# Moving operands of a matmul laid out line by line, three chunks interleaved, at a set distance from the weights

## What is computed

```python
# first block: T = 256 tokens, D = 2048
z = rmsnorm(x, g_mix) @ w_in                       # conv inputs, q, k, v, forget logits, gates
x = x + (gc * (conv_y @ w_conv_out) + ga * (attn @ w_attn_out)) @ w_mix_out
x = x + square(relu(rmsnorm(x, g_mlp) @ w_ff1)) @ w_ff2      # D_FF = 8192
x = rmsnorm(x, g_final)
# second block: shift, scale and gate come from silu(c) @ w_ada + b_ada
p = (rms_norm(x, g) * (1 + scale_m) + shift_m) @ w_in_2      # q, k, v, xs, z, B, C, dt
x = x + gate_m * (concat([rms_norm(moba_attention(q, k, v)), ssd_mixer(xs, z, B, C, dt)]) @ w_out_2)
h = rms_norm(x, g_ffn) * (1 + scale_f) + shift_f
x = x + gate_f * (conv_ffn(h, w_up, w_down))                 # FFN_DIM = 5632
out = rms_norm(x, g)
```

## Time and profile before

| | |
|---|---|
| time, median of 3 runs | 2489.05 us (2488.6 to 2489.89) |
| profiled execution | 2489.22 us, span 2487.4 us |
| TensorE (PE) busy | 2465.1 us, 99% |
| VectorE (DVE) busy | 1971.3 us, 79% |
| ScalarE (ACT) busy | 1263.9 us, 51% |
| mean granted TensorE clock | 0.999 |
| DMA | 567 MB, 228 GB/s over the span |

### The profile page before, as it was taken

The page is one execution under the profiler, slowest core; times in us unless marked ns, Lnnn a source line. Parts: engine busy times, 40 slices in busy tenths (PEclk is TensorE's granted clock), DMA queues, the critical chain, the costliest instruction groups (busy, mean ns, idle before and its releaser), DMA issues.

```text
span 2487.4 us, 46915 instructions
## 1 busy us (share of the span) xinstructions
PE 2465.1 (99%) x14373; PEld 2161.3 (87%) x14373; DVE 1971.3 (79%) x3113; ACT 1263.9 (51%) x2038; POOL 93.9 (4%) x109
## 2 busy tenths in 40 slices
PE   8999999999999999999999999999999999999998
PEld 7888888888888888888888888888888888888887
DVE  7778776689987887887888877776886886886886
ACT  5344445565554454444555555565544444445455
POOL 0000001000000000000000015300000000000000
PEclk9999999999999999999999999999999999999999
DMA  7786785557888888888888555555556656556554
GB/s 272 272 280 208 270 280 189 196 187 262 284 286 288 280 285 289 282 287 285 280 287 275 171 176 190 187 162 191 164 182 194 198 179 198 191 174 209 189 172 165
DMA packets 162668, 567.01 MB, mean 228 GB/s; under 512 B 18867, under 2 KB 19180, under 8 KB 162604
## 3 DMA queue, kind: packets, MB, share of 16 engines
q1 hardware_dynamic: 132428, 458.91, 55.6%
q10 hardware_dynamic: 27792, 101.20, 12.5%
q0 software_dynamic: 2384, 6.09, 1.0%
HBM read 563.70 MB, written 2.42 MB: 228 GB/s over the span
## 4 chain that ended last, share of the span: by engine, by line
PE 82%; DVE 2%; ACT 0%; issue 0%; DVEq 0%; POOL 0%; ACTq 0%; POOLq 0%
PE bank L302 82%; DVE w_lo L1306 0%; DVE Z L1666 0%; DVE H L1675 0%; ACT w_hi L789 0%; DVE scratch L1339 0%; PE bank L644 0%; PE bank L512 0%; DVE Z L2009 0%; ACT G L1118 0%; DVE scratch L1817 0%; PE bank L589 0%; DVE G L1789 0%; DVE scratch L1705 0%; PE bank L503 0%
## 5 line engine op out<-in xcount | busy, mean ns | idle before, releaser
L302 PE MATMUL bank<-H,w_hi 128*128 128x512 f32 (+1 forms) x4480 | 1395.5, 391 | 11.5 <-DVE w_lo L1368 9.4
L1306 DVE TENSOR_TENSOR w_lo<-w_raw,w_hi 128x1024 fp32r<-128x1024 f32 (+2 forms) x898 | 1047.9, 1176 | 124.6 <-ACT w_hi L789 114.4
L302 PEld LDWEIGHTS bank<-H,w_lo 128*128 128x128 f32 x4416 | 832.0, 188 | 178.4
L789 ACT ACTIVATE w_hi<-w_raw 128x1024 fp32r<-128x1024 f32 (+2 forms) x898 | 876.6, 1013 | 16.2 <-PE bank L302 8.8
L302 PE MATMUL bank<-H,w_lo 128*128 128x256 f32 x4416 | 876.6, 279 | 0.0
L302 PEld LDWEIGHTS bank<-H,w_hi 128*128 128x128 f32 x4480 | 686.6, 188 | 17.2 <-issue 13.7
L302 PE MATMUL bank<-U,w_hi 128*128 128x512 f32 (+1 forms) x2011 | 619.3, 389 | 0.0
L819 ACT ACTIVATE scratch<-bank 128x256 f32<-128x256 f32 x355 | 136.3, 384 | 721.7 <-PE bank L302 721.3
L302 PEld LDWEIGHTS bank<-U,w_lo 128*128 128x128 f32 x1984 | 371.6, 188 | 78.6
L302 PE MATMUL bank<-U,w_lo 128*128 128x256 f32 x1984 | 396.9, 279 | 0.0
L302 PEld LDWEIGHTS bank<-U,w_hi 128*128 128x128 f32 x2011 | 306.5, 188 | 2.8 <-DVE w_lo L1306 0.2
(11 more groups left out here) (243 smaller groups left out, 1120.0 us busy)
## 6 DMA issues: line engine op xcount, KB each, us to landing
w_raw<-in_w_ff SPq DMA_DIRECT2D x256, 512.0 KB, 5.0
ada_w<-in_w_ada ACTq DMA_DIRECT2D x192, 512.0 KB, 4.6
w_raw<-in_w_up SPq DMA_DIRECT2D x176, 512.0 KB, 4.3
w_raw<-in_w_z SPq DMA_DIRECT2D x96, 512.0 KB, 4.9
w_raw<-in_w_in SPq DMA_DIRECT2D x88, 512.0 KB, 4.2
w_raw<-in_w_gate SPq DMA_DIRECT2D x64, 512.0 KB, 4.7
w_raw<-in_w_down SPq DMA_DIRECT2D x64, 384.0 KB, 3.1
w_raw<-in_w_down SPq DMA_DIRECT2D x64, 320.0 KB, 3.4
```

Source lines behind the costliest of these rows:

```text
L302: return nc.tensor.matmul(out, lhsT, rhs, start=start, stop=stop, skip_group_check=True)
L789: A(w_hi[:, slot, 0:cols], w_raw[:, slot, 0:cols], ACT.Copy).then_inc(sem("w_high"), 1)
L1306: TT(w_lo[:, slot, 0:cols], w_raw[:, slot, 0:cols], w_hi[:, slot, 0:cols].bitcast(F32), ALU.subtract)\
```

## The change

- `H`, `U` and `B` are addressed through `chunks_by_line`. In place of 2048 bytes in a row a chunk is 128 lines of 16 bytes (4 elements), one every 48 bytes; chunk k begins 2048 bytes behind chunk k-1, so that three chunks interleave and together fill the space. One chain runs through all three buffers. It begins 16 bytes into the arena, which is 80 bytes past the weights' start, modulo 2048.
- All matmuls that read `H`, `U` or `B` (`mm_lines`), and all instructions that write or read them on ScalarE, VectorE and GpSimd, have access patterns of 64 or 128 lines of 4 elements. Their number, order and sizes stay.
- `H`, `U` and `B` no longer share memory with `G` and `Z` as before. To make room for this, the constants shrink from 1024 to 640 columns (the matrix `GT` is worked out by one VectorE subtraction into the mask's place; GpSimd's `mask_row` adds a 128-column mask to two thirds of a row), the last two G blocks move (`gates`), and the 352 columns of `ffn_w` and `ffn_b` are loaded later, over constants that are no longer needed.
- `small` moves ahead of `w_raw`, in the place of `spacing`.

```diff
-        U = nc.alloc_sbuf_tensor_at("U", [P, NC, 2 * T], F32R, offset=base)
-        G = nc.alloc_sbuf_tensor_at("G", [P, NC, 2, T], F32, offset=base)
-        Z = nc.alloc_sbuf_tensor_at("Z", [P, Z_BLOCKS, T], F32, offset=base + NC * 2 * T * 4)
-        B = nc.alloc_sbuf_tensor_at("B", [P, NC, 2 * T], F32R, offset=base + NC * 2 * T * 4)
+        def chunks_by_line(name, at):
+
+            area = nc.alloc_sbuf_tensor_at(name, [P, CHAIN_N], F32R, offset=base + at)
+            return bass.AP(area[:, :].tensor, LINE, [[CHAIN_N, P], [2 * T, NC], [STEP * LINE, LINES], [1, LINE]])
+
+        H = chunks_by_line("H", 0)
+        U = chunks_by_line("U", NC * 2 * T * 4)
+        B = chunks_by_line("B", 2 * NC * 2 * T * 4)
+        G = nc.alloc_sbuf_tensor_at("G", [P, NC, 2, T], F32, offset=base + NC * 2 * T * 4 + 4096)
+        Z = nc.alloc_sbuf_tensor_at("Z", [P, Z_BLOCKS, T], F32, offset=base + 2 * NC * 2 * T * 4 + 4096)
...
-        H = sb("H", [P, NC, 2 * T], F32R)
-        sb("spacing", [P, 48])
+        small = sb("small", [P, 496])
         w_raw = sb("w_raw", [P, 4, PIECE])
...
+        def lines(ap):
+            return ap.rearrange("p (l e) -> p l e", e=LINE)
+
+        def whole(buf, k):
+            return buf[:, k, :, :]
+
         def ob(buf, i, part):
 
-            return flat(buf[:, bass.ds(i, 1), part * T:(part + 1) * T])
+            at = slice(part * LINES // 2, (part + 1) * LINES // 2)
+            if isinstance(i, int):
+                return buf[:, i, at, :]
+            return buf[:, bass.ds(i, 1), at, :].rearrange("p a l e -> p (a l) e")
...
+            def mm_lines(out, lhsT, rhs, start, stop):
+                return mm(lines(out), lhsT, rhs, start, stop)
...
-                        return mm(dst[:, :], w_hi[:, 2 * par + h, c * P:(c + 1) * P], buf[:, k0 + c, :], start, False)
+                        return mm_lines(dst[:, :], w_hi[:, 2 * par + h, c * P:(c + 1) * P], whole(buf, k0 + c), start, False)
...
-                        return mm(dst[:, T:2 * T], w_lo[:, 2 * par + h, c * P:(c + 1) * P], buf[:, k0 + c, 0:T], False, stop)
+                        return mm_lines(dst[:, T:2 * T], w_lo[:, 2 * par + h, c * P:(c + 1) * P], ob(buf, k0 + c, 0), False, stop)
...
+            sp.wait_ge(sem("ssm.weights"), SSM_HEADS)
+            sp.dma_start(con[:, LEOL_AT:LEOL_AT + FFN_VEC_N], t["vectors"][:, VEC_N:VEC_N + FFN_VEC_N])\
+                .then_inc(sem("vec_landed"), 16)
...
-                A(ob(U, u, 0), wide[par], ACT.Square).then_inc(sem("u_high"), 1)
+                A(ob(U, u, 0), lines(wide[par]), ACT.Square).then_inc(sem("u_high"), 1)
...
-                        TT(ob(U, u, 1), conv[par], ob(U, u, 0).bitcast(F32), ALU.subtract).then_inc(sem("ff.u_ready"), 1)
+                        TT(ob(U, u, 1), lines(conv[par]), ob(U, u, 0).bitcast(F32), ALU.subtract).then_inc(sem("ff.u_ready"), 1)
...
+            TT(GT, ones[:, :], LE, ALU.subtract).then_inc(sem("sel_ready"), 1)
             channels_and_gate(0, split_ahead=True)
...
-                nc.gpsimd.tensor_tensor(key_bias[h % 2], key_bias[h % 2], MASK, ALU.add).then_inc(sem("at1.bias_ready"), 1)
+                diagonal = key_bias[h % 2].rearrange("p (n t) -> p n t", n=3)[:, 0:3:2, :]
+                nc.gpsimd.tensor_tensor(diagonal, diagonal, MASK.unsqueeze(1).to_broadcast([P, 2, P]), ALU.add).then_inc(sem("at1.bias_ready"), 1)
```

More of the change, by code:

```diff
@@ L59 @@
     _n += _size
-VEC_N = _n
-IDENT_AT, LEOL_AT, GT_AT, MASK_AT, CONST_N = 0, 128, 512, 640, 1024
+FFN_VEC_N = 264 + 88
+VEC_N = _n - FFN_VEC_N
+IDENT_AT, LEOL_AT, MASK_AT, CONST_N = 0, 128, 512, 640
+LINE = 4
+STEP = 3
+LINES = 2 * T // LINE
+CHAIN_N = NC * 2 * T + (STEP - 1) * 2 * T
 GROUP1 = 2 * FF_BLOCKS
@@ L134, in build @@
         scratch = sb("scratch", [P, 3072])
-        small = sb("small", [P, 496])
         mod = sb("mod", [P, 96])
@@ L218, in xb, with gates @@
             return flat(X[:, bass.ds(i, n), :])
+        def lines(ap):
+            return ap.rearrange("p (l e) -> p l e", e=LINE)
+        def whole(buf, k):
+            return buf[:, k, :, :]
         def ob(buf, i, part):
-            return flat(buf[:, bass.ds(i, 1), part * T:(part + 1) * T])
+            at = slice(part * LINES // 2, (part + 1) * LINES // 2)
+            if isinstance(i, int):
+                return buf[:, i, at, :]
+            return buf[:, bass.ds(i, 1), at, :].rearrange("p a l e -> p (a l) e")
+        def gates(m, par):
+            if isinstance(m, int) and m >= 14:
+                return zb(36 + 2 * (m - 14) + par)
+            return flat(G[:, bass.ds(m, 1), par, :])
         block = ctx.enter_context(nc.Block())
@@ L353, in joined_unit @@
                     high, low = (w[:, 2 + h, c * P:(c + 1) * P] for w in (w_hi, w_lo))
-                    steps = [(high, buf[:, k, 0:T]), (high, buf[:, k, T:2 * T]), (low, buf[:, k, 0:T])]
+                    steps = [(high, ob(buf, k, 0)), (high, ob(buf, k, 1)), (low, ob(buf, k, 0))]
                     for n, (lhsT, rhs) in enumerate(steps if c % 2 == 0 else steps[::-1]):
-                        end = mm(bank[1][:, 0:T], lhsT, rhs, k == 0 and n == 0, k == chunks - 1 and n == 2)
+                        end = mm_lines(bank[1][:, 0:T], lhsT, rhs, k == 0 and n == 0, k == chunks - 1 and n == 2)
                     if k in (cut - 1, chunks - 1):
@@ L454, in narrow @@
                 for k in range(NC):
-                    last = mm(bank[5][0:rows, :], w[:, k, :], H[:, k, :], k == 0, k == NC - 1)
+                    last = mm_lines(bank[5][0:rows, :], w[:, k, :], whole(H, k), k == 0, k == NC - 1)
                 last.then_inc(sem("soft.rows"), 1)
@@ L837, in first_chunks @@
                 for k in range(4 * i, 4 * i + 4):
-                    A(H[:, k, 0:T], X[:, k, :], ACT.Copy, scale=V("g_mix", k)).then_inc(sem("h_high"), 1)
+                    A(ob(H, k, 0), lines(X[:, k, :]), ACT.Copy, scale=V("g_mix", k)).then_inc(sem("h_high"), 1)
             for i in range(4):
@@ L916, in _ @@
                     act.sem_inc(sem("wait_over"), 1)
-                    A(ob(B, 2 * i + par, 0), wide[par], ACT.Copy).then_inc(sem("conv_mul.high"), 1)
+                    A(ob(B, 2 * i + par, 0), lines(wide[par]), ACT.Copy).then_inc(sem("conv_mul.high"), 1)
             with act.Fori(0, 3) as i:
@@ L955, in high @@
                     act.wait_ge(sem(name + ".mixed"), h + 1)
-                    A(ob(B, 8 + h, 0), bank[7][:, 0:256], ACT.Copy).then_inc(sem(name + ".high"), 1)
+                    A(ob(B, 8 + h, 0), lines(bank[7][:, 0:256]), ACT.Copy).then_inc(sem(name + ".high"), 1)
                 scale_q(0)
@@ L992, in _, with merge_units @@
             load_sigmoid()
-            with act.Fori(0, 8) as i:
+            def merge_units(i):
                 for par in range(2):
@@ L1008, in _ @@
                     act.sem_inc(sem("wait_over"), 1)
-                    A(ob(U, m, 0), conv[par], ACT.Copy).then_inc(sem("merged_high"), 1)
+                    A(ob(U, m, 0), lines(conv[par]), ACT.Copy).then_inc(sem("merged_high"), 1)
+            with act.Fori(0, 7) as i:
+                merge_units(i)
+            merge_units(7)
             c_sigmoid(1)
@@ L1070, in _ @@
                 act.wait_ge(sem("normed"), k + 1)
-                A(H[:, k, 0:T], zb(16 + k), ACT.Identity, bias=mod[:, k:k + 1]).then_inc(sem("h_high"), 1)
+                A(ob(H, k, 0), lines(zb(16 + k)), ACT.Identity, bias=mod[:, k:k + 1]).then_inc(sem("h_high"), 1)
             root("n3b")
@@ L1154, in ssm_high @@
                 act.wait_ge(sem("ssm.normed"), k + 1)
-                A(ob(B, k, 0), work(4 + k % 4), ACT.Copy).then_inc(sem("out2.high"), 1)
+                A(ob(B, k, 0), lines(work(4 + k % 4)), ACT.Copy).then_inc(sem("out2.high"), 1)
             def head_slot(i):
@@ L1183, in attn_high @@
                 act.wait_ge(sem("attn.normed"), h + 1)
-                A(ob(B, 8 + h, 0), attn_out[:, h, :], ACT.Copy).then_inc(sem("out2.high"), 1)
+                A(ob(B, 8 + h, 0), lines(attn_out[:, h, :]), ACT.Copy).then_inc(sem("out2.high"), 1)
             copy_values(N_HEADS - 1)
@@ L1257, in up @@
                     act.wait_ge(sem("up.act"), FFN_BLOCKS * g + i + 1)
-                    A(ob(U, i, 0), wide[0], ACT.Copy).then_inc(sem("u_high"), 1)
+                    A(ob(U, i, 0), lines(wide[0]), ACT.Copy).then_inc(sem("u_high"), 1)
                 up(0, cast_ahead=True, other=first)
@@ L1517, in finish @@
                     dve.wait_ge(sem(name + ".high"), h + 1)
-                    TT(ob(B, 8 + h, 1), bank[7][:, 0:256], ob(B, 8 + h, 0).bitcast(F32), ALU.subtract)\
+                    TT(ob(B, 8 + h, 1), lines(bank[7][:, 0:256]), ob(B, 8 + h, 0).bitcast(F32), ALU.subtract)\
                         .then_inc(sem(out_sem), 1)
@@ L1553, in _ @@
                     dve.wait_ge(sem("merged_high"), m + 1)
-                    TT(ob(U, m, 1), conv[par], ob(U, m, 0).bitcast(F32), ALU.subtract).then_inc(sem("merged"), 1)
```

(3 more changed lines are left out.)

60 lines of the change are left out of this document (32 added, 28 removed).

## The result

The changed kernel takes 2447.97 us (median of 4 runs, 2447.17 to 2448.28), 0.9835 of the time before, interval 0.9822 to 0.9848. So it is 41 us faster, where 117 us were forecast. The profiled execution took 2447.99 us with a span of 2446.2 us, at a mean granted clock of 0.999 as before. One thing in the chapters ahead needs a correction. They say that `H`, `U` and `B` no longer share memory with `G` and `Z` as before. `G` still lies over `U` and the first 4 KB of `B`, and `Z` over `B`, each 4096 bytes further on than the operand's start; only the start moved.

A forecast was written before the change was run, and what follows sets the result against it. TensorE's matmul pace was taken to bound the kernel. Moving reads gain 140 us, less 21 for the weight load and 2 for VectorE in the mix stage: 117 us off 2489.2 gives 2372 us, range 2345 to 2500 for 8 in 10.

The forecast's parts named there:

- What bounds the kernel: Whole kernel: it runs as fast as TensorE's matmuls follow each other; two pieces alone hold 65% of the span.
- The 140 and the 21 us: TensorE's pace: 140 us gained by moving the reads, less 21 us because loading weights of 128 columns bounds the pace too.
- the full gain: Likeliest case, in TensorE's matmul pace: another step between lines removes the loss; 2372 us, range 2345 to 2395, chance 0.45.
- So the step between lines must do the work, not the distance from the weights: Moving reads: inferred from 16-column weights giving 0.232 us per 512-column matmul, no faster than with 128 columns.
- A part of it: Rival: the step removes half the clashes, or low products keep their pace; 60 us, 2430 us, range 2395 to 2480, chance 0.20.
- No change: Rival: the loss comes from elsewhere, such as a 4-byte read limit whatever the line order; 2484 to 2494 us, chance 0.15.
- Slower: Rival: the changed kernel takes longer than the one before; chance 0.20.
- The terms at nothing: Operand writes on ScalarE and VectorE, `GT`, the added SyncE load and GpSimd's shorter mask: each taken as 0 or no cost.
- VectorE in the mix stage: Mix stage: VectorE busy 85.11 of 92 us, TensorE shrinking 5% to 87; with VectorE's waits, 2 us of gain left there.

The follow-up runs named there:

- the lone TensorE: Separate kernels where TensorE alone runs short matmul series in this kernel's pattern on filled operands; 2760 ns per 8 chunks at step 1, -192 bytes; 2716 at step 3, 80 bytes.
- The sweeps: TensorE-only series over steps, distances and weight widths; at step 1, 80 bytes, 2780 ns per 8 chunks with 16-column weights, 2800 with full ones.
- the run at the addresses of before: Changed kernel with step one and the chain's offset from one line to none, so stream at 128 and weights at 64 modulo 256; 2487.95 us, 0.9995 of before.

## Why the prediction was wrong in size

**What bounds the kernel** was read rightly. TensorE's pace is the time: six full kernels with mean paces of 2.7135, 2.759 to 2.761, 2.764 and 2.797 to 2.799 us took 2448, 2488 to 2489, 2490 and 2519 to 2523 us.

**The 140 and the 21 us** of the sum no run shows. In place of the 140, the lone TensorE shows a pace of 2.600 us in bfloat16, with 216 and 109 ns for the two widths, and 0.160 us x 864 = 138 us is what lay between it and the kernel before. In place of the 21 for the weight load, it shows float32r's low products at step 0 following at 110 to 113 ns and bfloat16's at 109 to 110; what the weight load has in that isn't shown.

**The step that failed** is the full gain, put at 0.45: its term of 140 us measured 41. A third of the loss goes, 47.5 of 160 ns for 8 chunks. The prediction took the loss for one thing that another order removes. The runs show two. The pace depends on the order of the stream's lines: with weights of 16 columns, at a distance of 0, 181 ns of 8 chunks are lost at step 1, 99 at step 3, 66 at the best order found. And it depends on where the stream stands against the weights: at step 3 it varies by 93 ns over the addresses. The two don't add up (before, with full weights, lost 160 ns, less than step 1 with narrow ones), so no share of the gain is put down to either alone. In the full kernel the step is worth 75 us with the weights at 64 and 28.5 us at 96, and at the addresses of before it would by the lone TensorE cost 12; with step 1 the new address costs 34 us. Only the pair gains.

**"So the step between lines must do the work, not the distance from the weights"** is the inference that fell. It rested on the earlier trace rows, matmuls with narrow weights that were no faster. The sweeps have the same: 2780 against 2800 ns at step 1. A partner that is taken away can show little where 180 ns are lost without it; and no row of before has full-width weights at another address to compare with (in the earlier trace rows `wn` is narrow and stands at another address, both at once). In the full kernel 32 bytes cost 42 us, where only buffers behind the stream, the weights among them, moved. In the lone TensorE the weights alone moved, from 64 to 96, and the pace went from 2712 to 2777 ns.

**The rivals.** *A part of it* came nearest: 2430 us, in a range of 2395 to 2480. That the step alone takes a part of the loss is half of the truth, since it had no word on the addresses. *No change* is out by 41 us. *Slower* is out too, and a cost by the bytes passed with it: steps of 17 and 19 lines (2760 to 2817 and 2720 to 2771 ns) cost what 1 and 3 cost. Yet a step that isn't chosen well would have been slower by far: step 6 takes 3.840 us for 8 chunks where the kernel before takes 2.760, and 864 x 1.08 is 933 us, an estimate. So its side was not unlikely.

**The terms at nothing** held: writers at 419, 419 and 474 ns where 418, 418 and 485 stood, 5.23 us for the 13 low halves in both, and the remaining edits together 0.9995 of before (0.9985 to 1.0005) by the run at the addresses of before. **VectorE in the mix stage**, 2 us, never came to bear, since TensorE's pace fell by 1.7% and not by 5%. The low products follow at 114 ns now and don't reach the 0.11 us of the earlier trace rows; at step 0 they do (110 to 113 ns).

**What stays open.** Which lines clash, and why steps 5, 6, 13 and 16 are so slow, isn't settled; the runs give a table and its period of 16 lines, not a map of the memory. That lines clash is a reading; what is measured is the pace against order, width and address. Why float32r's pace depends on the step where those of bfloat16 and plain float32, at 80 bytes and steps 1 and 3, don't (2600 and 5160 ns at both) isn't shown either, nor the 66 ns that remain at the best order, nor whether the layout with steps 3 and 4 keeps its gain in the full kernel.

## What to carry to other kernels

Where the profile shows TensorE busy for 99% and the matmuls of a 4-byte type follow each other slower than bfloat16 ones of the same columns (here 216 and 109 ns for 512 and 256), measure the pace against the addresses: shift the weights by 16 bytes at a time over 256, and try other steps between the lines of the moving operand. It takes one small kernel with TensorE alone, whose paces were those of the full kernel to a nanosecond or two in three cases and 8 ns off in a fourth. Read the addresses from the allocator and not from the edit: a tile 16 bytes longer moved the weights by 32, and a theory was dropped for it that the run in fact agreed with. And don't take one half of such a layout for the whole: here the address without the step cost 34 us, the step with the weights 32 bytes further on gave nothing against before, and no wait showed it.

## What the runs showed of the hardware that was not expected

- The pace of float32r matmuls depends on the order of the 16-byte lines, in the steps tried modulo 16 lines: 2632 ns for 8 chunks at step 0, 2716 at step 3, 2800 at step 1, 3200 at steps 5 and 13, 3467 at 16, 3840 at 6. No float32r series reached the 2600 ns of bfloat16.
- It depends on the distance between stream and weights, modulo 256 bytes, and less on the weights' own address: 2707 to 2800 ns at step 3, 2757 and more at step 1 in the pairs tried. In the full kernel 32 bytes were 42 us.
- The order of the lines and the weight load act together: steps 4 and 12 in turn, at a distance of 0, take 2667 ns with 16-column weights and 3067 with 128-column ones.
- Plain float32 took the same at 80 bytes and steps 1 and 3: 5160 ns for 8 chunks, in two records for each matmul, 215 to 216 ns apart at 256 columns.
- Loading the same weights, or reading the same moving chunk, again and again changes nothing (2814 and 2818 ns at step 1, 2717 and 2713 at step 3; the plain series gave 2800 and 2817, 2716 and 2713).
- ScalarE and VectorE write 16 bytes every 48 as fast as flat rows, 419 ns for 128x256 where flat ones took 418.
